# A sixteen-stage transformer kernel: weight slots converted in place, the last two output blocks by chunks, norm statistics with tokens on partitions, two opening blocks at once

## The reference

```python
def _layernorm(x, g, b):
    mu = jnp.mean(x, axis=-1, keepdims=True)
    var = jnp.mean(jnp.square(x - mu), axis=-1, keepdims=True)
    return (x - mu) * lax.rsqrt(var + LN_EPS) * g + b

def _swiglu(h, w_in, w_out):                       # F = 2816
    gate, up = jnp.split(h @ w_in, 2, axis=-1)
    return (jax.nn.silu(gate) * up) @ w_out

def _sublayer(x, fn, mod_j, g, b, weight):
    shift, scale, gate = mod_j                     # from silu(c) @ w_mod[i] + b_mod[i]
    y = fn(x * (1 + scale) + shift)
    return _layernorm(DEEPNORM_ALPHA * x + weight * gate * y, g, b)
```

## Time and profile before

| | us |
|---|---|
| time, median of 3 runs | 3140.94 (3140.32 to 3143.48) |
| the profiled execution's own time | 3138.93 |
| its span in the profile | 3137.1 |
| PE busy | 2776.5 (89%) |
| DVE busy | 2017.5 (64%) |
| ACT busy | 1265.3 (40%) |
| POOL busy | 1389.1 (44%) |
| DMA | 576.21 MB, mean 184 GB/s |

### The profile page before, as it was taken

How to read it: one execution, slowest core, us unless ns; L and a number is a source line. 1 busy time by engine, 2 the same in 40 slices (tenths; PEclk the granted TensorE clock), 3 DMA queues, 4 the chain that set the end, 5 groups by cost and what they waited for, 6 DMA issues and landing times.

```text
span 3137.1 us, 53378 instructions
## 1 busy us (share of the span) xinstructions
PE 2776.5 (89%) x20695; PEld 2656.6 (85%) x20695; DVE 2017.5 (64%) x2628; ACT 1265.3 (40%) x1667; POOL 1389.1 (44%) x1170
## 2 busy tenths in 40 slices
PE   3998889999976999999889999999879969779797
PEld 3998789999965999999764899999769969479797
DVE  6667776676658766666666666765876564764654
ACT  2444344344333444444332344443434434244443
POOL 0693958469383583793920079277670000000000
PEclk7998889999887898998975899899889989689898
DMA  8764557577472575764730377567445545034452
GB/s 298 252 249 144 189 202 252 202 240 260 148 247 71 198 254 180 255 256 158 235 120 0 108 254 267 176 231 271 151 142 173 176 155 177 14 111 131 134 185 83
DMA packets 357173, 576.21 MB, mean 184 GB/s; under 512 B 22256, under 2 KB 297899, under 8 KB 356907
## 3 DMA queue, kind: packets, MB, share of 16 engines
q1 hardware_dynamic: 357034, 574.29, 53.2%
HBM read 573.20 MB, written 1.05 MB: 183 GB/s over the span
## 4 chain that ended last, share of the span: by engine, by line
PE 70%; DVE 16%; issue 6%; POOL 4%; ACT 2%; DMA 1%; SPq 1%; DVEq 0%; POOLq 0%; ACTq 0%
PE ps L1553 64%; DVE wlo L1011 3%; POOL mod_acc L639 3%; PE ps L1873 1%; DVE acc L1126 1%; PE ps L1864 1%; DVE acc L1042 1%; DVE z L1142 1%; POOL mod_w L634 1%; ACT whi L654 1%; DVE std L1148 1%; DVE prob L1243 1%; PE ps L1694 1%; DVE hf L1155 1%; POOL mod_acc L630 1%
## 5 line engine op out<-in xcount | busy, mean ns | idle before, releaser
L1011 DVE TENSOR_TENSOR wlo<-raw,whi 128x1024 fp32r<-128x1024 f32 x804 | 1132.6, 1420 | 851.5 <-ACT whi L654 850.7
L654 ACT ACTIVATE whi<-raw 128x1024 fp32r<-128x1024 f32 x804 | 838.1, 1050 | 1227.9 <-PE ps L1553 1153.0
L1553 PE MATMUL ps<-H_hi,whi 128*128 128x256 f32 x4256 | 1230.3, 289 | 97.0 <-DVE H_lo L1160 37.6
L1553 PE MATMUL ps<-H_lo,whi 128*128 128x256 f32 x4256 | 1225.3, 288 | 0.0
L1553 PE MATMUL ps<-H_hi,wlo 128*128 128x256 f32 x4256 | 1224.3, 288 | 0.0
L1553 PEld LDWEIGHTS ps<-H_hi,whi 128*128 128x128 f32 x4256 | 839.6, 197 | 103.2 <-issue 85.3
L1553 PEld LDWEIGHTS ps<-H_lo,whi 128*128 128x128 f32 x4256 | 839.7, 197 | 0.1
L1553 PEld LDWEIGHTS ps<-H_hi,wlo 128*128 128x128 f32 x4256 | 838.8, 197 | 0.0
L639 POOL TENSOR_TENSOR mod_acc<-mod_acc,mod_w 128x512 f32<-128x512 f32 x462 | 792.3, 1743 | 0.0
L625 POOL TENSOR_TENSOR pool_tick<-cond 128x1 f32<-128x1 f32 x176 | 129.8, 738 | 952.9 <-DVE ax L1054 761.7
L1553 PE MATMUL ps<-A_hi,whi 128*128 (+1 forms) x1880 | 536.1, 285 | 16.0 <-DVE wlo L1011 12.9
(11 more groups left out here) (276 smaller groups left out, 2257.3 us busy)
## 6 DMA issues: line engine op xcount, KB each, us to landing
raw<-in_ffn_w_in_dram SPq DMA_DIRECT2D x176, 1024.0 KB, 5.1
mod_w<-in_w_mod_dram SPq DMA_DIRECT2D x180, 768.0 KB, 6.0
raw<-in_ffn_w_out_dram SPq DMA_DIRECT2D x88, 1024.0 KB, 6.5
raw<-in_w_gate_up_dram SPq DMA_DIRECT2D x22, 1024.0 KB, 5.1
raw<-in_ssm_w_in_dram SPq DMA_DIRECT2D x20, 1024.0 KB, 6.8
raw<-in_w_in_dram SPq DMA_DIRECT2D x14, 1024.0 KB, 5.0
raw<-in_diff_w_in_dram SPq DMA_DIRECT2D x12, 1024.0 KB, 7.0
raw<-in_w_down_dram SPq DMA_DIRECT2D x11, 1024.0 KB, 4.9
```

The costliest lines, as they stand in the source:

```text
L654: return nc.scalar.activation(dst, src, ACT.Copy)
L1011: tt(wlo[b % 2][:, r], raw[b % RAW][:, r], whi[b % 2][:, r].bitcast(F32), ALU.subtract).then_inc(w_lo, 1)
L1553: m = pe.matmul(out, l, r, start=first and i == 0, stop=last and i == 2, skip_group_check=rest)
```

## The change

**Slots.** Four slots hold raw, and `wlo` lies in the same memory: the subtract writes over its own input. `whi` has four slots too. A block is converted in one piece. The load of block b waits for PE to have finished block b - 4.

**Order of loads.** `mod_rows` says after which block of a stage each modulation unit is issued. The first two follow block 1 (the stage before has loaded that), and in a feed-forward one follows every second block from block 2 on.

**Ends and beginnings.** The last two blocks out are multiplied together, chunk by chunk (`ending`). The next stage's blocks 0 and 1 are both converted before the norm. The first two blocks in are multiplied together, as chunks of H arrive (`opening`).

**The norm.** ACT squares z before the centring, sums of z and of the squares run side by side, and products with one column give both sums with tokens on partitions (128 x 2). Mean, variance, root and reciprocal are taken there. A diagonal of the reciprocals times ones puts rstd on all partitions in PSUM, where `full` reads it. z times rstd, the gates, `ax` and its signal (`carry`) move into the next stage, behind the conversion of its block 2. Coefficients that don't depend on the modulation are computed once. The column sums of the modulation are taken in another order.

```diff
@@ SP
-            def load(b, it=None):
+            def load(b):
                 if b >= RAW:
-                    sp.wait_ge(w_lo, 2 * (b - RAW + 1) if it is None else 2 * (b - RAW + 1) + 8 * it)
+                    sp.wait_ge(products, plan.used[b - RAW][1])
...
+def mod_rows(kind):
+    if kind == "mla":
+        turns = [1, 1, 5, 6, 7, 8, 10] + 9 * [12]
+    elif kind == "diff":
+        turns = [1, 1] + [3 + 5 * j // 4 for j in range(8)] + 6 * [15]
+    elif kind == "ssm":
+        turns = [1, 1] + [2 + 3 * j // 2 for j in range(14)]
+    else:
+        turns = [1, 1] + [2 + 2 * j for j in range(14)]
...
+                    for i, b in enumerate(blocks):
+                        if b >= 2:
+                            load(b)
+                        for unit in after.get(i, []):
+                            load_mod(nxt, unit)
@@ slots
-        whi = [at(f"whi{i}", [P, SLOT], room(4 * SLOT), F32R) for i in range(2)]
-        wlo = [at(f"wlo{i}", [P, SLOT], room(4 * SLOT), F32R) for i in range(2)]
+        wlo = [at(f"wlo{i}", [P, SLOT], base + 4 * SLOT * i, F32R) for i in range(RAW)]
+        whi = [at(f"whi{i}", [P, SLOT], room(4 * SLOT), F32R) for i in range(RAW)]
@@ dve_ln
+                gated(0), gated(1), zsum(1)
+                gated(2), gated(3), zsum(2), zsum(3), sqsum(1)
+                gated(4), gated(5), zsum(4), zsum(5), sqsum(2), sqsum(3)
+                gated(6), zsum(6), sqsum(4), sqsum(5), sqsum(6)
+                gated(7), zsum(7), sqsum(7)
+                dve.wait_ge(s["ln_tok"], n["ln_tok"] + 1)
+                link(ts(tiny[:, 32:34], ps[:, 6, S + 16:S + 18], 1.0 / D, None, ALU.mult))
...
+                link(nc.vector.reciprocal(tiny[:, 40:42], tiny[:, 38:40]))
+                for t in range(ST):
+                    i = ts(std[:, 0, t * P:t * P + P], ident, tiny[:, 40 + t:41 + t], None, ALU.mult)
+                i.then_inc(s["diag"], 1)
...
+            def carry(st):
...
+                dve.wait_ge(s["rstd_out"], ln.n["rstd_out"] + 1)
...
+                    i = tt(z[:, r, :], z[:, r, :], rstd, ALU.mult)
+                gates(sub + 1, ln.n)
+                residual(LNA[:, 0, 8 * sub:8 * sub + 8], LNA[:, 1, 8 * sub:8 * sub + 8])
@@ dve_ffn, turn
                     convert(g.b + i + 2, it)
+                    if i == 0 and it is None:
+                        carry(st)
@@ pe_ln
-                    mod_sums(0, 5, False)
+                    mod_sums(8, 12, False)
                 pe.wait_ge(s["zsum"], n["zsum"] + 7)
+                for t in range(ST):
+                    m = pe.matmul(ps[:, 6, S + 16 + t:S + 17 + t], acc[:, 0, t * P:t * P + P], ones[:, 0:1], start=True, stop=True)
...
                 if more:
-                    mod_sums(5, 16)
-                folded(n, "ln_var")
+                    mod_sums(12, 16, False)
+                    mod_sums(0, 8)
+                pe.wait_ge(s["diag"], n["diag"] + 1)
+                pe.matmul(ps[:, 5, S:2 * S], ones, std[:, 0, :], start=True, stop=True).then_inc(s["rstd"], 1)
                 if more:
                     mod_sums(16, 24)
```

More of the change, by code:

```diff
@@ L182 @@
 }
+UNITS = 2 * DC
+def mod_rows(kind):
[7 more added lines that the diff above has]
+        turns = [1, 1] + [2 + 2 * j for j in range(14)]
+    after = {}
+    for u, t in enumerate(turns):
+        after.setdefault(t, []).append(u)
+    return after
 class Step:
@@ L975, in act_post @@
                         .then_inc(s["y_sq"], 1)
-                finish(g)
+                for c in (6, 7):
+                    act.wait_ge(products, ready(g, c))
+                    i = nc.scalar.activation(sq[:, c, :], ybank(g, c), ACT.Square)
+                i.then_inc(s["y_sq"], 1)
                 ready_table(ACT.Sqrt)
@@ new lines, in dve_ln @@
+                i.then_inc(s["diag"], 1)
+                if st.kind == "ln":
+                    coefficients(sub + 1, n)
+                    dve.wait_ge(s["rstd"], n["rstd"] + 1)
+                    full(0), full(1), centre(2), low(0), full(2), low(1), full(3), low(2), centre(3), full(4), low(3)
+                    for c in range(5, DC):
+                        full(c), low(c - 1)
+                    low(DC - 1)
+                    return
+                centre(2), centre(3)
+                dve.wait_ge(s["rstd"], n["rstd"] + 1)
@@ new lines, in columns @@
+                wait_split(b, 0, it)
+                order = [(h, c, k) for h in range(2) for c in range(2) for k in range(4 * h, 4 * h + 4)]
+                if first:
+                    order = [(k // 4, c, k) for k in range(DC) for c in range(2)]
+                for j, (h, c, k) in enumerate(order):
+                    if first and c == 0:
+                        whole(first, k)
+                    if between and j == DC:
+                        between()
+                    o = ps[:, bank(p) + c, 0:S]
+                    if tokens:
+                        t = slice(c * P, c * P + P)
+                        m = three(o, b % RAW, k * 256, 256, x_hi[:, k, t], x_lo[:, k, t], k == 0, k == 7, swap=True)
+                    else:
+                        m = three(o, b % RAW, k * 256 + c * P, P, x_hi[:, k, :], x_lo[:, k, :], k == 0, k == 7)
+                    if j % DC == DC - 1:
+                        m.then_inc(products, 1)
@@ new lines, in whole, with opening @@
+            def whole(st, k):
+                pe.wait_ge(s["h_lo"], st.n["h_lo"] - st.parts + k * st.parts // DC + 1)
+            def opening(st, g):
+                for i in range(2):
+                    wait_banks(g.p + i)
+                    wait_split(g.b + i, 0)
+                for k in range(DC):
+                    whole(st, k)
+                    for i in range(2):
+                        for c in range(2):
+                            m = three(ps[:, bank(g.p + i) + c, 0:S], (g.b + i) % RAW, k * 256 + c * P, P, H_hi[:, k, :], H_lo[:, k, :],
+                                      k == 0, k == 7)
+                            if k == DC - 1:
+                                m.then_inc(products, 1)
@@ L1591, in turn @@
                     b = g.b + i
-                    last = it is None and i == g.n - 1
+                    if it is None and i == g.n - 2:
+                        ending(b)
+                    if it is None and i >= g.n - 2:
+                        return
+                    order = [(h, c) for h in range(2) for c in range(DC)]
                     if i == 0:
@@ L1799, in read, with row @@
                     pe.wait_ge(banks_free[p % 2], plan.free_val[p])
-            def row(g, x_hi, x_lo, tokens=False, wait=None):
-                for i in range(g.n):
-                    columns(g, i, x_hi, x_lo, None, tokens, wait if i == 0 else None)
+            def row(g, x_hi, x_lo, tokens=False, first=None):
+                if first:
+                    opening(first, g)
+                for i in range(2 if first else 0, g.n):
+                    columns(g, i, x_hi, x_lo, None, tokens)
             def fin_sums(n, first=None):
@@ L1821, in pe_ssm @@
                 L = st.lin
-                row(L["z"], H_hi, H_lo, wait=(s["h_lo"], n["h_lo"] - 4))
+                row(L["z"], H_hi, H_lo, first=st)
                 row(L["xbc"], H_hi, H_lo)
@@ L1939, in pe_xatt @@
                 L = st.lin
-                for i in range(L["q"].n):
-                    columns(L["q"], i, H_hi, H_lo, wait=(s["h_lo"], n["h_lo"] - 4) if i == 0 else None)
+                opening(st, L["q"])
+                for i in range(1, L["q"].n):
+                    if i > 1:
+                        columns(L["q"], i, H_hi, H_lo)
                     if i == 1:
```

332 lines of the change are left out of this document (152 added, 180 removed).

## The result

The changed kernel takes 3268.57 us (median of 4 runs, 3266.8 to 3271.76) against 3140.63 for the kernel before beside it (3133.11 to 3143.48): a ratio of 1.0412 (1.0407 by the two medians), 95% interval [1.0392, 1.0433]. It is slower by 128 us; 3275 was forecast. The span grew from 3137.1 to 3264.9 us, so the profiles explain 127.8.

What follows compares the result with a forecast made beforehand. PE bounds the kernel (busy 89% of the span), so time moves only where PE stands still. Norms 21 + 5.5, opening 3, holds 79, feed-forward 0 2, MLA 18, diff 1, ssm 6: 135.5 on 3138.93, rounded to 3275 us; range 3235 to 3315.

Steps and rivals of the forecast that it cites:

- The hold before block 3: Feed-forwards 2, 3, 5, 6, 8, 9: load 3 queued behind modulation unit 2, which waits for POOL; 13.2 us each, +79.
- The step that chose POOL's unhindered 2.03 us: POOL's unit 0 in the hold: 2.03 us with a 0.2 tick, because DVE sits waiting for block 3.
- The norm: Gap from last to first dense product: 19.2 us against 16.2, DVE's z sums late; +21 after seven feed-forwards.
- MLA: Two MLA stages: POOL ends 3 us later, and the end costs 6 us more; +18 for both.
- State space: State space stage: norm +3; held load 5 in the z phase and convolutions +1 to +5, together +6.
- Differential attention: Differential attention stage: norm behind it +2.5, and block 4 held until S'+31.6 but earlier paced by POOL, +1.
- Feed-forward 0: First feed-forward: has its ax early, so only +2 there, beside its norm (+3.0) and opening (0.4).
- The opening: First two blocks multiplied together in eight feed-forwards: block 2 waits 0.4 us for ACT's gate, +3 in all.
- Norms short: Rival, chance 0.15: block 1 early or DVE's sums no bound, norm gap T+11, load still held; 3184 us.
- Load not held: Rival, chance 0.07: block 3's load in feed-forwards is not held, norms stay long; 3188 us.
- Not slower: Rival, chance 0.10: DVE up to date, sums at 2.4 GHz, gap 7.4, -93, holds at lower bound; 3112 us.
- The queue is too short: Rival, chance 0.06: loads take over 11 us beside modulation loads, every second block waits; 3440 us.

Runs made afterwards that it cites:

- x1: Changed kernel with modulation unit 2 issued behind the load of block 5 instead of block 2 in feed-forwards: 3185.22 us, ratio 1.0155.
- x2: Changed kernel with modulation unit 2 issued behind the load of block 3 instead of block 2 in feed-forwards: 3240.46 us, ratio 1.0333.
- x6: Changed kernel with carry ahead of the subtract of block 2 instead of behind it in feed-forwards: 3253.44 us, ratio 1.0381.
- x3: Changed kernel with DVE subtracting block 1 of the next stage behind the norm's diagonals instead of ahead of the first z: 3241.10 us, ratio 1.0334.
- x5: Changed kernel with block 1 of the next stage subtracted behind the diagonals (DVE) and copied behind the eighth square (ACT): 3223.35 us, ratio 1.0277.
- x4: Changed kernel with PE taking twelve column sums of the modulation (24 records) before it waits for the last z sum: 3230.48 us, ratio 1.0302.
- x12: x11 with the next stage's first two loads between units 14 and 15 in MLA, instead of behind unit 15: 3096.23 us, ratio 0.9870.
- x7: x1 with the first two blocks of feed-forwards multiplied one after the other instead of together: 3185.18 us, ratio 1.0161.
- x11: Changed kernel plus x4, x5, conversions in halves, unit 2 behind block 5 (feed-forwards, state space) or block 4 (differential attention): 3090.02 us, ratio 0.9849.
- x10: Changed kernel with x1, x5 and x4 together, conversions whole and other loads as they were: 3131.84 us, ratio 0.9972.

## Why the prediction came out

**The hold before block 3** was forecast at 13.2 us for each of six feed-forwards, 11.4 of waiting and 1.8 of slow clock, and the stages grew by 11.8 without their norms. Waiting was 9.5 to 10.6, and five small errors are in it. In feed-forward 3 `ax` came 1.4 us early (at 14.0; the forecast's own terms add up to 15.6, not 15.4) and the load took 7.0 us and not 7.8; POOL and the queue took 0.7 longer, and copy, subtract and product 5.85 instead of 5.05, as the subtract took 3.15 beside POOL. So block 3 started 0.7 early. Block 2 ended at 20.3 us and not 19.1, mostly because 26 products and not 15 ran at a pitch of 0.213 us after the start. x1 shows the whole of it, x2 moves it by one block, x6 shortens it by its first link. The step that chose POOL's unhindered 2.03 us was right here, and x2 shows its reason: when DVE's subtract falls into it, the unit takes twice as long. The sentence on shared interfaces of POOL and VectorE (the Trainium skill, GPSIMD Engine Reference, Specifications) agrees with 4.06 against 2.03.

**The norm** was forecast at 19.2 us and measured at 18.9 to 19.9 after feed-forwards. That it came out so close is luck: inside, two errors cancel. The last z sum came at 6.9 us and not 8.4, since block 1 landed 5.2 us after its issue at 627.20, not 6.4. From there to the first product I had 10.8 us (the terms as printed add up to 11.1) and the trace has 12.0, all of it on PE: 2.6 for the sums over tokens, 5.1 for the 24 records, 1.0 for rstd and 3.3 for the 16 records behind it. The sum had those 16 at nothing, though they are the last line of the third order excerpt, and put 1.9 us of DVE's work in their place, which was done 1.1 us before the first product. x3 and x5 show the subtract in front, which was named, and ACT's copy, which was not: I had given the whole lateness to DVE. x4 shows the 24 records. I had DVE's diagonal ready 3 us early; it was 3.3.

**MLA** was forecast at +18 for two and measured at +18.5, by another split. POOL ended 129.2 us after the first product (131 forecast; 128.2 before) and PE waited only 1.24 us for it. The end of the stage took 8.9 us more than before, not 6: the blocks landed at 405.4 and 408.4, the second just as POOL ended (408.45) and not 1.5 us before, and DVE was free 4.3 us past POOL's end, not 2.8. (The expectation of x12 has 402.8 and 405.4 for these landings; that is 3 us too early.) PE's wait at L1724 is 12.1 us there, the longest of its row. The term was right in sum and mis-sized in both parts.

**State space** was forecast at +9 and measured at +13.5 in this profile, and at +7.4 to +8.1 in x1, x2, x6 and x7, which leave the stage alone. The hold is 9.68 us here (9.0 to 9.3 there) and not 5, so what came out was a sum: I had let later blocks absorb half of it. In x11, where it is gone together with the old order of the stage's units, the stage is shorter by more than the hold; whether the blocks behind it absorb any is not shown. **Differential attention** was forecast at +3.5 and measured at -2.2: its norm gap was 13.4 us, since the last z sum came 2.9 us past the product and the token sums then still ran at the 2.4 GHz level (0.60 us for four records against 1.01). Under kernels that left its code alone the gap was 13.1 to 17.4, so one profile says little of it. **Feed-forward 0** was forecast at +5.4 and came to +4.9. **The opening** was forecast at 0.4 us a stage; x1 less x7 is 0.45 on average in the profiles. **The norms between pre and post** and the rest were forecast at +1 and came to +3.

Sum: 135.5 forecast, 127.8 measured. The six feed-forwards outside their norms are 8 us under the 79 of the holds. The other errors, up to 6 us each way, cancel, and that is luck; the two large terms, holds and norms, have the causes that were named, the norms only in part.

**The rivals.** *Norms short* needs the gap at 11: it stayed at 19. *Load not held* falls with the row at 674.49. *Not slower* was wrong because all three of its conditions failed: DVE up to date, sums at 2.4 GHz, holds at the bottom (they cost 11.8 and not 9.6). x10 and x11 show that its mechanism is half sound: with DVE 2.9 us behind the last product and the sums early, the gaps after feed-forwards are 2.3 to 4.2 us shorter than the old ones, but 12.0 to 13.5 us long and not 7.4. *The queue is too short* falls: in x1 PE waits in no feed-forward once the first product has started, with every load issued only when the slot's block has been multiplied.

## What to carry to other kernels

A queue in program order holds everything behind its first waiting instruction, so a transfer whose release comes from a slow chain must stand behind all those that will be wanted before the chain can be done; count from the chain's start, not from the transfer's size. Work for the next stage that an engine does ahead of a reduction is not free because the next stage is far off: put it where the engine waits inside the reduction, on every engine that touches it. And small products on TensorE belong into its idle time ahead of a wait, where they run at the higher clock as well; once that wait is short they delay what stands behind them (x10: 3.3 us a norm gained alone, 1.4 together with x5). Last, gains of single runs add up only as far as each is read from the stage that it changes.
